# A hybrid attention and mixture-of-experts layer: keys loaded ahead, output weights in halves, and another order of the token tiles

## What is computed

```python
h = rmsnorm(x, g_norm_mix) * (1 + sc1) + sh1
y_a = dsa_attention(qa, ka, va, qi, ki, wi)   # a query sees up to 256 keys, chosen by score
y_b = retention(qb, kb, vb, gb, positions)
x = x + gt1 * (concat(y_a, y_b) @ w_o)
h = rmsnorm(x, g_norm_ffn) * (1 + sc2) + sh2
x = x + gt2 * hier_moe(h, ...)                # the router picks 2 of 32 experts for each token
return rmsnorm(x, g_norm_final)
```

## Time and profile before

| | us |
|---|---|
| runs shown (3) | 1712.06, 1718.81, 1719.7 |
| median of them | 1718.81 |
| the profiled execution's own time | 1713.41 |
| its span in the trace | 1711.5 |
| TensorE busy | 1473.0 (86% of the span) |
| VectorE busy | 1125.3 (66%) |
| ScalarE busy | 912.8 (53%) |
| GpSimd busy | 286.1 (17%) |

### The profile page before, as it was taken

The page is one execution under the profiler, slowest core; times in us unless marked ns, Lnnn a source line. Parts: engine busy times, 40 slices in busy tenths (PEclk is TensorE's granted clock), DMA queues, the critical chain, the costliest instruction groups (busy, mean ns, idle before and its releaser), DMA issues.

```text
span 1711.5 us, 21563 instructions
## 1 busy us (share of the span) xinstructions
PE 1473.0 (86%) x7406; PEld 1149.6 (67%) x7406; DVE 1125.3 (66%) x1496; ACT 912.8 (53%) x1228; POOL 286.1 (17%) x212
## 2 busy tenths in 40 slices
PE   3899998999999897778899752999999999999940
PEld 2587445888887785455666542788888888888830
DVE  6633778662267973334444235899999999999936
ACT  4321665879983112324444301677777777777711
POOL 0000100240000001400000001223223232232125
PEclk8899989999999898599999965999999999999975
DMA  9198532222323226112211104999999999999847
GB/s 370 46 340 316 197 131 105 99 99 99 117 71 128 79 68 222 52 50 74 75 50 44 50 25 148 391 397 398 404 399 398 398 398 400 392 403 395 346 163 269
DMA packets 103990, 368.27 MB, mean 215 GB/s; under 512 B 11248, under 2 KB 24176, under 8 KB 79344
## 3 DMA queue, kind: packets, MB, share of 16 engines
q1 hardware_dynamic: 75632, 291.85, 44.7%
q10 hardware_dynamic: 17024, 41.95, 6.4%
q0 software_dynamic: 11264, 33.57, 5.5%
HBM read 306.50 MB, written 69.21 MB: 220 GB/s over the span
## 4 chain that ended last, share of the span: by engine, by line
PE 74%; DVE 11%; DMA 5%; ACT 4%; issue 3%; POOL 2%; SPq 1%; DVEq 0%; POOLq 0%; ACTq 0%
PE PS L1618 19%; PE PS L1620 19%; PE PS L1619 18%; PE PS L1719 3%; PE PS L1920 2%; PE PS L1743 2%; DMA WK<-in_w_ada 1%; PE PS L1829 1%; PE PS L1816 1%; DVE wlo L1541 1%; DVE WK L1045 1%; PE PS L1704 1%; PE PS L1675 1%; DMA BIG<-in_b_sh 1%; PE PS L1895 1%
## 5 line engine op out<-in xcount | busy, mean ns | idle before, releaser
L1541 DVE TENSOR_TENSOR wlo<-raw,whi 128x2048 fp32r<-128x2048 f32 x192 | 435.9, 2286 | 33.9 <-ACT whi L958 33.5
L958 ACT ACTIVATE whi<-raw 128x2048 fp32r<-128x2048 f32 x192 | 363.9, 1914 | 116.2 <-DVE WK L1560 80.8
L1618 PE MATMUL PS<-whi,xhi 128*128 128x512 f32 x512 | 203.8, 398 | 7.3 <-DVE wlo L1541 6.5
L1620 PE MATMUL PS<-whi,xlo 128*128 128x512 f32 x512 | 201.1, 393 | 0.0
L1619 PE MATMUL PS<-wlo,xhi 128*128 128x512 f32 x512 | 200.1, 391 | 0.0
L850 ACT ACTIVATE KV<-ACC,WK 128x1024 int8<-128x1024 f32 (+4 forms) x160 | 147.5, 925 | 29.9 <-DVE WK L1181 27.3
L1618 PE MATMUL PS<-KVR,BIGR 128*128 128x512 f32 x320 | 127.7, 399 | 5.9 <-DVE KVR L1107 5.9
L699 POOL COPY wcol<-tw 128x1 f32 (+1 forms) x32 | 63.0, 1969 | 376.8 <-DVE WK L1578 376.8
L1620 PE MATMUL PS<-KVR,BIGR 128*128 128x512 f32 x320 | 125.4, 392 | 0.0
L1619 PE MATMUL PS<-KVR,BIGR 128*128 128x512 f32 x320 | 125.0, 391 | 0.0
L1618 PEld LDWEIGHTS PS<-whi,xhi 128*128 128x128 f32 x512 | 97.0, 189 | 27.6 <-issue 5.7
(11 more groups left out here) (322 smaller groups left out, 2966.3 us busy)
## 6 DMA issues: line engine op xcount, KB each, us to landing
raw<-in_w_gate SPq DMA_DIRECT2D x64, 1024.0 KB, 7.8
raw<-in_w_up SPq DMA_DIRECT2D x64, 1024.0 KB, 7.8
raw<-in_w_down SPq DMA_DIRECT2D x64, 1024.0 KB, 7.2
y_dram<-zero ACTq DMA_DIRECT2D x8, 3072.0 KB
WK<-in_w_ada POOLq DMA_DIRECT2D x16, 1024.0 KB, 7.4
y_dram<-WK ACTq DMA_DIRECT2D x32, 512.0 KB
KV<-in_w_in SPq DMA_DIRECT2D x5, 2048.0 KB, 9.8
KV<-in_x SPq DMA_DIRECT2D x16, 512.0 KB, 5.0
```

Source lines behind the costliest of these rows:

```text
L958: nc.scalar.activation(whi[:, slot], raw[:, q], ACT.Copy).then_inc(G("m_hi"), 1)
L1541: V.tensor_tensor(wlo[:, slot], raw[:, q], whi[:, slot].bitcast(F32), ALU.subtract)\
L1618: mm(out_, x_hi, w_hi, start=first, stop=False)
L1620: return mm(out_, x_lo, w_hi, start=False, stop=final)
```

## The change

- The order of the tiles is 3, 0, 4, 1, 5, 2, 6, 7 (`TILES`); queries, retention rows, x, x1, xn and the router's results follow it.
- The keys move to the place of chunk ka's rounded weights, and are loaded whole in SP's step 17 of retention; `keys0` goes.
- w_o is loaded in two halves, k = 4 to 7 when the last projection is done, k = 0 to 3 after the last retention values and behind gt1. Its rounding moves from quarters 0 to 3 to quarters 2 to 5, in the order 4, 5, 6, 7, 0, 1, 2, 3. GpSimd subtracts k = 4 to 7; VectorE subtracts k = 0 to 3 in quarters 4 and 5, that is, in the first two quarters of the second position.
- gt1 has a semaphore of its own. Late sums 0 and 1 move to the third and fourth quarter of the first position, 2 to 5 to the second position, 6 and 7 (gt2) from position 7 to position 5; gt2 is loaded at position 3.
- The selection is drained before the first masks.

```diff
@@ -38,8 +38,8 @@
...
 NEG_LOGIT = -1.0e30
-KEY_PARTS = ((0, 512), (512, 1024))
-KEYS_FROM = {128: 0, 256: 1, 640: 2}
+TILES = (3, 0, 4, 1, 5, 2, 6, 7)
+WO_ORDER = (4, 5, 6, 7, 0, 1, 2, 3)
 SMALLEST = 2.0 ** -126
@@ -159,12 +163,11 @@
...
         wo_lo = BIGR[:, 8192:16384].rearrange("p (k c) -> p k c", k=KD)
-        wo_hi = [BIGR[:, a:a + 1024] for a in (0, 1024, 2048, 3072, 20480, 21504, 22528, 23552)]
-
         KV = sb_before("KV", [P, 8192 + 2048])
-        kaT = KV[:, 0:4096].rearrange("p (j s) -> p j s", j=4)
+        kaT = BIG[:, 20480:24576].rearrange("p (j s) -> p j s", j=4)
         va = BIG[:, 16384:20480].rearrange("p (t c) -> p t c", t=T)
         kiD = KV[:, 8192:9216]
+        wo_hi = [(BIGR, WOR)[k // 4][:, 1024 * (k % 4):1024 * (k % 4) + 1024] for k in range(KD)]
         xall = KV[:, 0:8192].rearrange("p (t d) -> p t d", t=T)
@@ -380,11 +382,12 @@
...
                        [("turn", i - 1)]] for i in range(3, T)}
-        between[0] = [[("late", m)] for m in range(4)]
-        between[1] = [[("late", 4)], [("late", 5), ("mix", (0, 0))], [("mix", (0, 1))], [("norm", 0)]]
+        between[0] = [[], [], [("late", 0)], [("late", 1)]]
+        between[1] = [[("late", 2)], [("late", 3), ("mix", (0, 0))], [("late", 4), ("mix", (0, 1))],
+                      [("late", 5), ("norm", 0)]]
         between[2] = [[("turn", 0), ("mix", (1, 0))], [("route", 0), ("mix", (1, 1))], [("norm", 1)], [("turn", 1)]]
-        between[T - 1][2].append(("late", 6))
-        between[T - 1][3].append(("late", 7))
+        between[5][2].append(("late", 6))
+        between[5][3].append(("late", 7))
         between[T] = [[("route", T - 2)], mix(T - 1), [("norm", T - 1), ("turn", T - 1)], [("route", T - 1)]]
@@ -507,7 +510,7 @@
...
             def load_queries(n):
-                sp.dma_start(queries(n), q_dram[:, :, tile(n)]).then_inc(G(f"ld_q{n % 2}"), 16)
+                sp.dma_start(queries(n), q_dram[:, :, tile(TILES[n])]).then_inc(G(f"ld_q{n % 2}"), 16)
@@ -530,6 +533,11 @@
...
                         .then_inc(G(f"st_q{n % 2}"), 16)
+                if step == 2 * T + 1:
+                    for q in range(2):
+                        sp.wait_ge(G(f"st_q{q}"), 16 * T)
+                    sp.wait_ge(G("a_proj"), T * (ATTEND + 2))
+                    sp.dma_start(kaT, k_dram).then_inc(G("ld_k0"), 16)
                 if step == T:
@@ -539,19 +547,15 @@
...
-            for q in range(2):
-                sp.wait_ge(G(f"st_q{q}"), 16 * T)
-            sp.dma_start(keys0, k_dram[:, :, 0:P]).then_inc(G("ld_k0"), 16)
             sp.wait_ge(G("a_proj"), UNITS)
-            for n, (a, b) in enumerate(KEY_PARTS):
-                sp.dma_start(kaT[:, :, a:b], k_dram[:, :, a:b]).then_inc(G(f"ld_k{n + 1}"), 16)
-            sp.dma_start(wo, wo_v).then_inc(G("ld_wo"), 16)
+            sp.dma_start(wo[:, 4:8], wo_v[:, 4:8]).then_inc(G("ld_wo"), 16)
             sp.wait_ge(G("b_y"), T)
-            sp.dma_start(WC["gt1"], b_gt1).then_inc(G("ld_c"), 16)
-            sp.dma_start(WC["wr"], w_router).then_inc(G("ld_c"), 16)
+            sp.dma_start(WC["gt1"], b_gt1).then_inc(G("ld_gt1"), 16)
+            sp.dma_start(wo[:, 0:4], wo_v[:, 0:4]).then_inc(G("ld_wo_last"), 16)
             sp.dma_start(WC["sc2"], b_sc2).then_inc(G("ld_c"), 16)
...
             sp.dma_start(WC["sh2"], b_sh2).then_inc(G("ld_c"), 16)
+            sp.dma_start(WC["wr"], w_router).then_inc(G("ld_c"), 16)
             store_retained(T - 1)
@@ -560,21 +564,20 @@
...
                     sp.wait_ge(G("c_ytr"), i)
-                sp.dma_start(WC["yb"], yb_dram[tile(i), :]).then_inc(G("ld_yb"), 16)
+                sp.dma_start(WC["yb"], yb_dram[tile(TILES[i]), :]).then_inc(G("ld_yb"), 16)
...
-                sp.dma_start(WC["x"], x_v[i]).then_inc(G("ld_xr"), 16)
-                if i == T - 1:
-                    sp.wait_ge(G("topk_done"), len(SCORED))
+                sp.dma_start(WC["x"], x_v[TILES[i]]).then_inc(G("ld_xr"), 16)
+                if i == 3:
                     sp.dma_start(gt2, b_gt2).then_inc(G("ld_gt2"), 16)
@@ -670,8 +673,8 @@
...
-            for k in range(KD):
-                pool.wait_ge(G("w_hi"), 4 * (ATTEND + 3) + k + 1)
+            for k in range(4, KD):
+                pool.wait_ge(G("w_hi"), 4 * (ATTEND + 3) + WO_ORDER.index(k) + 1)
                 own.go(tt(wo_lo[:, k], wo[:, k], wo_hi[k].bitcast(F32), ALU.subtract), G("wo_lo"))
@@ -918,9 +921,10 @@
...
                             exponent(v)
-                    if i == 0:
-                        for k in (lo, lo + 1):
-                            act.wait_ge(G("ld_wo"), 16)
+                    quarter = 4 * i + lo // 2
+                    if 2 <= quarter < 6:
+                        for k in WO_ORDER[2 * quarter - 4:2 * quarter - 2]:
+                            act.wait_ge(G("ld_wo" if k >= 4 else "ld_wo_last"), 16)
                             own.go(A(wo_hi[k], wo[:, k], ACT.Copy), G("w_hi"))
@@ -1251,8 +1255,9 @@
...
                 i = u // HA
-                K = cols_of(i)
-                bias = WC["bias01"][:, 256 - K:256] if i < FIRST_SCORED else ACC[:, ACC_OFF[i]:ACC_OFF[i] + K]
+                n = TILES[i]
+                K = cols_of(n)
+                bias = WC["bias01"][:, 256 - K:256] if n < FIRST_SCORED else ACC[:, ACC_OFF[n]:ACC_OFF[n] + K]
                 b = 2 * (u % 2)
@@ -1351,6 +1356,7 @@
...
                 if step == 3 * T - 1:
+                    spend(1000.0, pieces)
                     negated_logits(0)
@@ -1358,17 +1364,20 @@
...
                     spend(STEP_SPEND, pieces)
-            for _ in pieces:
-                pass
-
...
                         negated_logits(u)
+                    quarter = 4 * i + lo // 2
+                    if 4 <= quarter < 6:
+                        for k in (2 * quarter - 8, 2 * quarter - 7):
+                            dve.wait_ge(G("w_hi"), 4 * (ATTEND + 3) + WO_ORDER.index(k) + 1)
+                            own.go(V.tensor_tensor(wo_lo[:, k], wo[:, k], wo_hi[k].bitcast(F32), ALU.subtract),
+                                   G("w_lo"))
                 if kind == "late":
                     row, h = LATE[i // 2][0], i % 2
-                    dve.wait_ge(*((G("ld_gt2"), 16) if row == "gt2" else (G("ld_c"), 16 * 5)))
+                    dve.wait_ge(*((G("ld_" + row), 16) if row in ("gt1", "gt2") else (G("ld_c"), 16 * 4)))
                     part = slice(512 * h, 512 * h + 512)
@@ -1728,12 +1737,11 @@
...
-                K = cols_of(i)
+                K = cols_of(TILES[i])
                 if lo == 0:
+                    if i == 0:
+                        pe.wait_ge(G("ld_k0"), 32)
                     pe.wait_ge(G(f"ld_q{i % 2}"), 16 * (i // 2 + 1))
-                    if cols_of(i) in KEYS_FROM:
-                        n = KEYS_FROM[cols_of(i)]
-                        pe.wait_ge(G(f"ld_k{n}"), 32 if n == 0 else 16)
                 if HA * i + lo >= 2:
@@ -1879,7 +1887,10 @@
...
                         if i == 0 and h == 0:
-                            pe.wait_ge(G("wo_lo"), k + 1)
+                            if k < 4:
+                                pe.wait_ge(G("w_lo"), 4 * (ATTEND + 3) + k + 1)
+                            else:
+                                pe.wait_ge(G("wo_lo"), k - 3)
                         last = split_product(PS[:, 7, :], yhi[:, k, :], ylo[:, k, :], wo_hi[k][:, part], wo_lo[:, k, part],
```

More of the change, by code:

```diff
@@ L151, in block_kernel @@
         rounded.close()
+        rounded = ExitStack()
+        rounded.enter_context(nc.sbuf_tensor("BIGP", [P, 24576], F32R))
+        WOR = rounded.enter_context(nc.sbuf_tensor("WOR", [P, 4096], F32R))[:, :]
+        rounded.close()
         BIG = sb_before("BIG", [P, 24576])
@@ L408, in groups @@
         def groups(i):
-            return (i + 4) // 4
+            return (TILES[i] + 4) // 4
         def pt_index(i, h, g):
@@ L1743, in query_keys @@
                         last = mm(PS[:, 2 * (h % 2) + b, 0:w], queries(i)[rows, h // 2, :],
-                                  (kaT if i else keys0)[rows, h // 2, 512 * b:512 * b + w], start=True, stop=True)
+                                  kaT[rows, h // 2, 512 * b:512 * b + w], start=True, stop=True)
                         if w < 512 or 512 * b + w == K:
@@ L1814, in turn_weights @@
                     pe.wait_ge(G("c_pt"), n - 1)
-                for b in range(4 * g, min(4 * g + 4, i + 1)):
+                for b in range(4 * g, min(4 * g + 4, TILES[i] + 1)):
                     last = tr(PS[:, 4 + n % 2, P * (b % 4):P * (b % 4) + P],
@@ L1892, in _ @@
                     bank7(("route", i, 0))
-                    pe.wait_ge(G("ld_c"), 16 * 5)
+                    pe.wait_ge(G("ld_c"), 16 * 4)
                     for k in range(KD):
```

17 lines of the change are left out of this document (8 added, 9 removed).

## The result

| | before | after |
|---|---|---|
| median of 4 runs each, us | 1717.97 | 1702.68 (1701.88 to 1706.63) |
| the profiled execution's own time, us | 1713.41 | 1701.88 |
| its span, us | 1711.5 | 1700.1 |

The ratio of the times is 0.9916, with a 95% interval of 0.9893 to 0.9940: 10 to 18 us faster. The forecast was 1702.7. The sum behind it gave 1697.3 for a profiled execution, which took 1701.88; 5.4 us were then added for the way from the profiled execution to the median, which is 0.8 here.

What follows compares the result with a forecast made beforehand. Two stalls on constants and one slow-clock stretch in attention were taken as winnable. Terms sum to -16.1 us, from 1713.41 to 1697.3 for a profiled execution; forecast median 1702.7, lying 5.4 higher; range 1689 to 1714.

Steps and rivals of the forecast that it cites:

- Term a: First position, tile 3 for tile 0: heads of the second position at 701.5 us, -5.2 us; clock returns in quarter 2.
- the clock stays up: Rival: clock stays up or returns at once; first position 4.7 us less, first output half 2.45 less, 1695.5 us; chance 0.20.
- Term b: Second position, tile 0 with four late sums and half the splitting: 39.3 us for 36.3, +3.0 us.
- Term c: Third to eighth positions with tiles exchanged, late sums in the sixth included: -3.1 us.
- Tile 4 third: Part of Term c: tile 4 in the third position takes 38.6 us, against its 37.9 before.
- Tile 1 fourth: Part of Term c: tile 1 in the fourth position takes 31.3 us, with TensorE idle some 3 us.
- tile 2 sixth: Part of Term c: tile 2 in the sixth position takes 35.5 us, including 1.7 for two late sums.
- the slower rival: Small tiles lower the clock in fourth and sixth positions; half clock throughout the fourth alone adds 23 us, 1725.7; chance 0.05.
- Term d: Eighth position without the wait for gt2: row sums follow the turn at once, -9.4 us.
- Term e: Last row sums, transposes after them and start of the product, no longer at half clock after idling: -1.4 us.
- The collision: Rival: VectorE's four subtractions each wait out a GpSimd one, 9.4 us before the first output product; 1712.1 us; chance 0.11.
- Selection drained, keys ahead, weights in halves at no cost: Before the first masks: draining the selection, loading keys early and halving the output weights cost nothing.

Runs made afterwards that it cites:

- e2: Kernel before the change, with only gt2 loaded at position 3 and its two late sums moved from position 7 to 5; ratio to before 0.9962, median 1711.03 us.
- e7: Kernel before the change, with only a semaphore of its own for gt1, the first layer norm table row; ratio to before 0.9966, median 1711.79 us.
- e12: Changed kernel with natural tile order, all subtractions on GpSimd, rounding in quarters 1 to 4, unused matmuls filling TensorE's early gaps; ratio to before 0.9853, 1692.96 us.
- e10: Changed kernel, tile 3 still first, with added unused matmuls in TensorE's gaps of the first position and three quarters of the second; ratio to before 0.9908, 1700.26 us.
- e4: Changed kernel with all eight output weight subtractions back on GpSimd, none on VectorE; ratio to before 0.9901, median 1698.45 us.
- e11: Changed kernel with the output weights' rounding back in quarters 0 to 3, all else as changed; ratio to before 0.9907, median 1699.19 us.
- e3: Changed kernel with the keys loaded late again, after the last projection and ahead of the output weights; ratio to before 0.9944, median 1706.72 us.
- e1: Changed kernel with the tiles back in natural order 0 to 7, all else as changed; ratio to before 0.9878, median 1696.37 us.
- e9: e5 with added unused matmuls in TensorE's gaps of the first position and first three quarters of the second; ratio to before 0.9879, median 1695.39 us.
- e5: Changed kernel with natural tile order and all eight subtractions on GpSimd; ratio to before 0.9878, median 1698.29 us.

## Why the prediction was right, and where it was not

**The median was met by luck, the direction by reasoning.** The sum of the terms was -16.1 us, nearly all of it in the stage; the two traces differ by 11.4: 1.3 from an earlier entry, which no term had, 9.7 in the stage, 0.4 in the tail. Median against median it is 15.3. Stage and median do not always agree: e2's are 6.5 and 5.6 us shorter than before, the change's 9.7 and 15.3, e7's 3.0 and 6.7, e12's 22.3 and 25.5. The executions without a trace may differ in the stage or outside it; that stays open.

**Term a (first position, -5.2): right in kind, measured -7.5** with the entry taken out (heads of the second position at 697.89 for 706.67, entry 1.30 earlier). The clock fell and came back in quarter 2 as said. The working priced each quarter by TensorE, which the trace bears out: 6.6, 6.2 and 5.5 us for 7.3, 7.4 and 5.9. It doubled rows at full clock and summed them, where the rows at half clock took 2.08 and 1.97 us and overlap a little, and so came out 2.3 us high. The rival "the clock stays up" was to give 7.2 us, 4.7 of them in the first position; e10 measures 3.1 in the stage, 0.1 of them there, but its added matmuls delay the first position by some 4 us, so that it does not decide on the 4.7.

**Term b (second position, +3.0): measured +4.6** (697.89 to 738.82, 40.9 us, for 36.3). The chain of rounding, subtraction and pick-up ran as worked out, and the first product stood 45.0 us after the first key product, where 47.3 was forecast. The second product was 1.6 us of miss: it began in full clock, fell back during its first matmuls, and took 7.4 us for 5.8. e4 and e11 show what the step left unsaid, that this chain of waits was a cost of the change which either edit avoids.

**Term c (third to eighth, -3.1 with +1.7 of late sums in it): the step that missed most.** Without the late sums it promised -4.8. Order and gt2 together gave -6.9, gt2 alone -6.5 (e2): the order gave 0.4. These six positions, with term d, were to take 12.5 us less and took 6.9 less. Tile 4 third was right (38.7 for 38.6). Tile 1 fourth took 34.4 us for 31.3, tile 2 sixth 36.5 for 35.5, the eighth position 43.7 for 42.1. In the fourth the clock fell: the router product took 2.39 us for 1.98 and the mix behind it 8.3 for 5.8, 2.9 of the 3.1 us missed. Windows of seven microseconds of the first mix, in the kernel after and in the one before:

```profile
785.00:792.00 7.00, 6.62 (x18) 5.21 (x19) 0.20 (x1) 0.00 (x0) 0.00 (x0) 0.56 0.00 0
```

```profile
785.00:792.00 7.00, 6.62 (x34) 5.40 (x33) 0.20 (x1) 0.00 (x0) 0.00 (x0) 1.00 0.00 0
```

TensorE is busy 6.62 us in both, with 18 matmuls in one and 34 in the other. I had this as the slower rival, at half clock throughout and 23 us a position, and as a bound of 0 to +4 for the fourth position, of which I took 0. What sets the fall off is not settled. From the row sums to that mix TensorE was busy 6.04 of 8.20 us here and 6.87 of 9.10 before, nearly the same share. And the sixth position of the changed kernel and of e4 have the same work with the same waits, up to a mix that runs at half clock in the first and at full clock in the second:

```profile
852.84 0.63 PE L1872 MATMUL PS<-cst,WK 128*128 128x128 f32 x4 [0.65 <-ACT WK L947]
...
854.95 0.87 PE L1824 MATMUL PS<-cst,WK 128*128 128x128 f32 x6 [0.64 <-DVE WKR L1403]
856.46 0.88 PE L1837 MATMUL PS<-WK,BIG 128*64 128x128 f32 x12 [0.63 <-ACT WK L920]
...
859.62 0.77 PE L1627 MATMUL PS<-BIGR,WKR 128*128 128x512 f32 x1 [0.38 <-DVE L L1430]
```

```profile
851.34 0.63 PE L1866 MATMUL PS<-cst,WK 128*128 128x128 f32 x4 [0.65 <-ACT WK L947]
...
853.46 0.87 PE L1818 MATMUL PS<-cst,WK 128*128 128x128 f32 x6 [0.64 <-DVE WKR L1397]
854.97 0.88 PE L1831 MATMUL PS<-WK,BIG 128*64 128x128 f32 x12 [0.63 <-ACT WK L920]
...
858.12 0.48 PE L1621 MATMUL PS<-BIGR,WKR 128*128 128x512 f32 x1 [0.38 <-DVE L L1424]
```

The two differ in what came before. At the start of the fifth position both are at half clock, but the changed kernel is back at full clock in the first of these key products and e4 only near their end:

```profile
814.99 1.60 PE L1751 MATMUL PS<-BIG,KV 64*128 64x512 f32 x8
```

```profile
812.12 2.93 PE L1745 MATMUL PS<-BIG,KV 64*128 64x512 f32 x8
```

So e4 pays in the fifth position (40.48 us for 39.11) and the changed kernel in the sixth (36.53 for 35.06). The sum of the two is the same: 75.5 and 75.6 us, as in e3, e10 and e11 (75.6, 75.6, 75.7). Gaps of this kind cost the clock somewhere, but from the gap alone it can't be told where. The Trainium skill (TensorE: Matmul & The Clock Gate, "A second HAM failure mode") tells of a kernel whose small idles between groups of matmuls make the clock swing and pay each time; here that happens with waits of 0.4 to 1.1 us, at 1.4 to 2.5 us a time.

**Term d (gt2, -9.4): measured -7.9** in the eighth position (e2). The step assumed that the turn keeps its place: it came 1.6 us later, because the clock fell at the start of the position. In e1, where it did not fall there, the position took 9.5 us less than before, so the stall itself was sized rightly.

**Term e (tail, -1.4): measured -1.0** from the start of the last row sums to the first product behind them (4.4 us for 5.4), of which the row sums are 0.9 (1.09 us for 1.98). To the end of the span only 0.4 of it is left.

**The collision** of GpSimd's and VectorE's subtractions did not come: VectorE's four took 1.18 us each (2.36 the pair), as single passes do; they began at 701.23 us, GpSimd's ended at 698.6. It can be seen in e4, where a 512-column pass that takes 0.69 us alone took 2.33 beside GpSimd's, behind the pick-up for which the mix waits, so that it decided nothing there. VectorE's timeline of e4:

```profile
707.36 2.33 DVE L1380 TENSOR_TENSOR BIG<-BIG 128x512 f32<-128x512 f32 x1
```

The rule of the Trainium skill (SBUF — State Buffer, "Who interferes with whom"), that a VectorE instruction with two SBUF inputs and a GpSimd one that reads SBUF exclude each other, agrees with that row.

**Selection drained, keys ahead, weights in halves at no cost:** nothing before the stage got longer, and the last table landed 12.3 us after its issue for 15.5. What I did not price is that the keys' early load saves the 4 to 5 us of e3 once tile 3 is at the front.

## What to carry to other kernels

Price a stretch by the engine whose work ends last in it, and look for who waits for whom before naming it. An experiment that adds work to hold the clock up also delays what stands behind that work: here the granted clock of the first position rose from 0.56 to 0.92 and its length fell by 0.3 us, which at first looked as if the clock did not matter, while the added matmuls had held up ready work for some 4 us. A reordering that leaves TensorE small waits ahead of a long product should carry a charge for the clock, here 1.4 to 2.5 us a time; in which position it is paid was not predictable. And where several edits are made at once, undo each alone: the order cost 5.6 us of stage in a change that shortened it by 9.7, and nothing in the total showed it.

## What was not expected of the hardware

Matmuls whose result nobody reads, 256 columns of the identity's product in gaps of 0.3 to 5 us, held the granted clock at 1.00 from 675 to 720 us in e9, where the same kernel without them (e5) had 0.50 up to 710 us. They left the first position's length alone (21.2 for 21.5 us), where they also held up ready work, and with the earlier rounding took 5.4 us off the traced stage (299.9 to 294.5). The medians of the two kernels, as ratios 0.9856 and 0.9853, do not show it.
